# One-hots of the expert slots on two engines, and gate products that start on half of their input

## The reference, cut to what matters

```python
D_MODEL = 1024; N_EXPERT_GROUPS = 4; EXPERTS_PER_GROUP = 8; EXPERT_TOP_K = 2; D_EXPERT = 128
def hier_moe(h, ...):
    pg = softmax(h @ w_rg + b_rg); gi = argmax(pg); gp = pg[gi]
    le_sel = (h @ w_re + b_re).reshape(N, 4, 8)[gi]
    top_p, top_i = lax.top_k(softmax(le_sel), 2)
    top_p = top_p / sum(top_p)
    gates = gp * one_hot(gi) * sum_k(top_p * one_hot(top_i))
    a = einsum('nd,edf->nef', h, w_gate)
    b = einsum('nd,edf->nef', h, w_up)
    hid = silu(a) * b * gates
    return einsum('nef,efd->nd', hid, w_down)
```

## Time and profile before

| | |
|---|---|
| three runs, median | 427.64 us (425.98 to 429.17) |
| profiled execution, its own time | 425.02 us |
| its span | 423.1 us |
| busy: PE | 385.6 us (91%) |
| busy: PEld | 208.2 us (49%) |
| busy: DVE | 214.1 us (51%) |
| busy: ACT | 151.1 us (36%) |
| busy: POOL | 70.4 us (17%) |
| moved by DMA | 109.17 MB, mean 258 GB/s |
| chain that ended last | PE 81%, DVE 8%, DMA 4%, issue 3%, ACT 3% |

### The profile page before, as it was taken

How to read it: one execution, slowest core, us unless ns; L and a number is a source line. 1 busy time by engine, 2 the same in 40 slices (tenths; PEclk the granted TensorE clock), 3 DMA queues, 4 the chain that set the end, 5 groups by cost and what they waited for, 6 DMA issues and landing times.

```text
span 423.1 us, 6421 instructions
## 1 busy us (share of the span) xinstructions
PE 385.6 (91%) x2466; PEld 208.2 (49%) x2466; DVE 214.1 (51%) x442; ACT 151.1 (36%) x321; POOL 70.4 (17%) x59
## 2 busy tenths in 40 slices
PE   0998999979998999999989999879999999998692
PEld 1454544434443434446443466766556555553470
DVE  2967599697457456447361354651212222222276
ACT  5725022222464365454351356312212222222053
POOL 0000546443100100000000001221333233211000
PEclk9999999999999999999999999999999999999698
DMA  8991845892605033960039998999999999995484
GB/s 287 354 279 45 306 136 162 267 352 79 202 0 201 14 114 123 286 214 1 2 104 415 410 412 326 357 352 403 401 409 410 412 408 405 409 394 211 139 323 198
DMA packets 42323, 109.17 MB, mean 258 GB/s; under 512 B 7864, under 2 KB 8632, under 8 KB 42288
## 3 DMA queue, kind: packets, MB, share of 16 engines
q1 hardware_dynamic: 36000, 94.79, 60.7%
q0 software_dynamic: 5856, 12.81, 8.0%
q10 hardware_dynamic: 432, 1.11, 0.8%
HBM read 100.00 MB, written 16.94 MB: 276 GB/s over the span
## 4 chain that ended last, share of the span: by engine, by line
PE 81%; DVE 8%; DMA 4%; issue 3%; ACT 3%; POOLq 0%; DVEq 0%; ACTq 0%
PE bank L1576 34%; PE bank L1890 13%; PE bank L1909 6%; PE bank L1550 4%; PE bank L1879 3%; PE bank L1836 3%; DMA tokens_split<-h_rows,middle 3%; PE bank L1625 3%; PE bank L1617 3%; PE bank L1639 3%; PE bank L1768 2%; PE bank L1672 2%; PE bank L1944 2%; DVE weights_split L1044 2%; PE bank L1699 1%
## 5 line engine op out<-in xcount | busy, mean ns | idle before, releaser
L1576 PE MATMUL bank<-weights_split,tokens_split 128*128 128x512 f16 (+1 forms) x648 | 149.0, 383 | 1.5 <-DVE x L1288 1.4
L1576 PEld LDWEIGHTS bank<-weights_split,tokens_split 128*128 128x128 f16 (+1 forms) x648 | 61.2, 97 | 79.8 <-issue 10.4
L655 POOL TENSOR_TENSOR big<-big,middle 128x1536 f32<-128x1536 f32 x8 | 27.8, 3474 | 64.0 <-DMA middle<-sample_q 41.7
L1890 PE MATMUL bank<-big,tokens_split 128*64 128x256 f32 x320 | 36.7, 382 | 1.5 <-ACT tokens_split L968 1.5
L1471 DVE TENSOR_TENSOR middle<-bank,middle 128x128 f32<-128x128 f32 x16 | 4.7, 292 | 53.7 <-ACT middle L973 53.7
L1890 PEld LDWEIGHTS bank<-big,tokens_split 128*64 128x64 f32 x320 | 23.0, 137 | 12.5 <-ACT tokens_split L968 2.0
L1836 PE MATMUL bank<-half_consts 128*128 128x256 f16 x186 | 23.5, 291 | 4.4 <-issue 4.4
L702 POOL DMA_INDIRECT expert_rows<-weights_split,middle x16 | 16.0, 1002 | 65.9 <-PE bank L1879 42.4
L1550 PE MATMUL bank<-ident,big 128*128 128x128 f32 (+1 forms) x92 | 14.6, 294 | 12.2 <-DVE big L1054 9.5
L844 ACT ACTIVATE middle<-bank 128x128 f32<-128x128 f32 (+3 forms) x32 | 13.9, 435 | 29.5 <-PE bank L1625 29.3
L1836 PEld LDWEIGHTS bank<-half_consts 128*128 128x128 f16 x186 | 19.1, 104 | 8.7 <-issue 5.5
(11 more groups left out here) (199 smaller groups left out, 544.8 us busy)
## 6 DMA issues: line engine op xcount, KB each, us to landing
big<-in_w_gate SPq DMA_DIRECT2D x10, 1024.0 KB, 12.3
big<-in_w_up SPq DMA_DIRECT2D x10, 1024.0 KB, 16.7
big<-in_w_down SPq DMA_DIRECT2D x10, 1024.0 KB, 18.5
middle<-in_w_in SPq DMA_DIRECT2D x16, 512.0 KB, 7.0
big<-in_cache_win_k SPq DMA_DIRECT2D x24, 256.0 KB, 4.5
middle<-in_cache_win_v SPq DMA_DIRECT2D x24, 256.0 KB, 4.5
big<-in_w_out SPq DMA_DIRECT2D x8, 512.0 KB, 7.2
big<-expert_rows SPq DMA_DIRECT2D x8, 512.0 KB, 6.6
```

The costliest lines, as they stand in the source:

```text
L655: nc.gpsimd.tensor_tensor(prod[:, :, :], kring[:, b % 2], qb[:, b % 2, :].unsqueeze(1).to_broadcast([P, NPAT, W]), ALU.mult).then_inc(prod ...
L1576: ins = T.matmul(out, (hT if rows is None else rows)[:, high_low, k if rows is None else k - 4, tokens], wg[:, place, part, k, columns], s ...
L1890: ins = T.matmul((ptb, ovb)[b][e * CAP:(e + 1) * CAP, 0:2 * FE], xT[:, b, k, e * CAP:(e + 1) * CAP], places[slot][:, 0:2, e, k * FE:(k + 1 ...
```

## The change

Four edits belong together.

- **Slot codes.** An odd expert's code is now `1000 * par + rk` (`ODD = 1000`). The row compared with it is 0 to 63 in its first half and 1000 to 1063 in its second. A token with a rank of 64 or more then matches nothing by itself, and the two instructions that added 1000 to it are gone. The row is now written with two instructions in the place of one, during attention.
- **One-hots.** VectorE compares for `kt` = 0 to 6. For 7, 8 and 9 ScalarE computes |code - row| and then max(0, 1 - that), which is 1 where they are equal and 0 elsewhere, since both are whole numbers. The second instruction waits for the first. TensorE's last three small products wait for ScalarE's semaphore.
- **ScalarE's copy** of the first four transposed pieces waits for the fourth transpose (`half_turned`), not for the eighth.
- **Gate products** of chunks 0 to 3 wait for ScalarE's copy only; the wait for VectorE's copy stands ahead of chunk 4.

```diff
+BY_COMPARE, ODD = 7, 1000
...
+            act.wait_ge(slots_ready, 1)
+            for i, kt in enumerate(range(BY_COMPARE, 2 * NT)):
+                hot = onehot_p[:, kt, :]
+                nc.scalar.activation(hot, iota_h, ACT.Abs, scale=-1.0, bias=r1[:, kt:kt + 1]).then_inc(onehots_a, 1)
+                act.wait_ge(onehots_a, 2 * i + 1)
+                nc.scalar.activation(hot, hot, ACT.Relu, scale=-1.0, bias=1.0).then_inc(onehots_a, 1)
+
             def copy_x(n, b):
 
-                act.wait_ge(turned, n + 1)
+                act.wait_ge(half_turned, n + 1)
                 nc.scalar.activation(xT[:, b, 0:4, :], sbk[0][:, :].rearrange("p (k c) -> p k c", k=4),
                                      ACT.Copy).then_inc(xt_a, 1)
...
-                    V.tensor_copy(iota_h, iota[:, 0:P])
+                    V.tensor_copy(iota_h[:, 0:CAP], iota[:, 0:CAP])
+                    V.tensor_scalar(iota_h[:, CAP:P], iota[:, CAP:P], float(ODD - CAP), None, ALU.add)
...
             step(V.tensor_reduce(rk, OX, AX, ALU.add))
-            V.tensor_scalar(r2, rk, float(CAP), 1000.0, ALU.is_ge, ALU.mult)
-            step(V.scalar_tensor_tensor(out=r1, in0=par, scalar=float(CAP), in1=rk, op0=ALU.mult, op1=ALU.add))
-            step(V.tensor_tensor(r1, r1, r2, ALU.add))
+            V.scalar_tensor_tensor(out=r1, in0=par, scalar=float(ODD), in1=rk, op0=ALU.mult,
+                                   op1=ALU.add).then_inc(slots_ready, 1)
+            dve.wait_ge(slots_ready, 1)
 
             def slots():
 
-                for kt in range(2 * NT):
+                for kt in range(BY_COMPARE):
                     V.tensor_scalar(onehot_p[:, kt, :], iota_h, r1[:, kt:kt + 1], None, ALU.is_equal).then_inc(onehots, 1)
...
-                    pe.wait_ge(onehots, kt + 1 if part == 0 else 2 * NT + 1)
+                    if part == 0 and kt >= BY_COMPARE:
+                        pe.wait_ge(onehots_a, 2 * (kt - BY_COMPARE + 1))
+                    else:
+                        pe.wait_ge(onehots, kt + 1 if part == 0 else BY_COMPARE + 1)
...
                 for k in range(KD):
                     ins = T.transpose(sbk[k // 4][:, (k % 4) * P:(k % 4 + 1) * P], xg[:, b, k * P:(k + 1) * P], ident[:, :])
+                    if k == 3:
+                        ins.then_inc(half_turned, 1)
                 ins.then_inc(turned, 1)
 
             def gate_up(base, j):
 
                 n, b, slot = base + j, j % 2, j % SLOTS
                 pe.wait_ge(xt_a, n + 1)
-                pe.wait_ge(xt_d, n + 1)
                 pe.wait_ge(gu_in[slot], base * (2 * LOADS[slot]) + 32 * (j // SLOTS + 1))
                 for k in range(KD):
+                    if k == 4:
+                        pe.wait_ge(xt_d, n + 1)
                     for e in range(2):
```

More of the change, by code:

```diff
@@ L408, in build @@
         zeroed = sem("zeroed")
+        half_turned, slots_ready, onehots_a = sem("half_turned"), sem("slots_ready"), sem("onehots_by_scalar")
         diags_set, rows_gated = sem("diags_set"), sem("rows_gated")
@@ L1429, in more_tables @@
                 step(V.tensor_scalar(hi, xi, 6, None, ALU.logical_shift_right), dv_more)
-                V.scalar_tensor_tensor(out=slot_no, in0=par, scalar=float(CAP), in1=lo, op0=ALU.mult, op1=ALU.add)
+                V.scalar_tensor_tensor(out=slot_no, in0=par, scalar=float(ODD), in1=lo, op0=ALU.mult, op1=ALU.add)
                 step(V.scalar_tensor_tensor(out=r4, in0=hi, scalar=float(PAIRS), in1=pair_no, op0=ALU.mult, op1=ALU.add), dv_more)
```

## The result

Side by side on one chip, 22 runs of each, the changed kernel takes a median of 426.38 us (424.19 to 431.29) and the kernel before 429.13 us (425.34 to 430.75). The ratio is 0.995, with a 95% interval of 0.9927 to 0.9973: 0.5% of 429.13, some 2.1 us less. The two medians themselves lie 2.75 us apart: they count all executions, while every ratio leaves out those over 1.5% above the fastest of their kernel, the slow ones (here two of the changed kernel's, none of the other's). The time lies in the predicted range and within 1%, but the forecast had a gain of 0.2 us. The two profiled executions are 425.02 and 424.58 us, only 0.44 us apart. So there are two questions: why the path gave 0.44 us, and where the other 1.7 us come from. The second is answered in part only.

The account below looks back on a forecast made before the run. The prediction took the router's end as one chain and the full DMA weight stream as holding the last pair: 0.09 at the table and 0.47 made 0.56 us, the stream left 0.25, so 427.64 - 0.2 = 427.4 us, range 425.5 to 429.0.

Parts of the forecast that it names:

- Slot codes and one-hots: Router's end: VectorE's one-hots end at 277.25, ScalarE's last at 277.96, so the table copy starts 0.09 us earlier.
- Rival 2: Router's end: ScalarE's one-hots end after VectorE's did, table 0.29 to 0.6 us later, 427.9 to 428.2 us; chance 0.17.
- The prediction's second estimate: ScalarE's one-hots by the Trainium skill's figures: 0.62 us a one-hot and a table gain of 0.08 us.
- Gate products after half: First two pairs: copying after the fourth transpose starts gate products 0.47 us earlier for pair 0, 0.94 for pair 1.
- What is late next: Gather for pair 3: its issue moves by pair 0's 0.47 only, so TensorE goes on 0.56 us earlier.
- rival 1: Weight stream: it has room, so the first pairs' gain arrives, 0.56 us (427.1) or 1.03 us (426.6); chance 0.26.
- What the stream lets through: Last pair: the weight stream holds its gate products, so 0.25 us of the 0.56 us gain is left.
- TensorE being early adds no byte: Weight stream: after its first loads the DMA engines are full, so the loads move only by the table's 0.09 us.
- The sum: Whole program: profiled execution of 425.02 us less 0.25 us gives 424.8 us.
- The median: Median of three runs, 427.64, lies 2.6 us above the profiled execution most likely through the stream; less 0.2 gives 427.4.
- The likeliest case: Whole program: the forecast itself, with the stream holding the last pair and 427.4 us; chance 0.53.
- the chances by 1%: Whole program: time within 1% (4.3 us) of the kernel before 0.94, faster 0.04, slower 0.02.

Follow-up runs that it names:

- half_only: Kernel before with ScalarE's copy started after the fourth transpose, gate products still waiting for both copies; one run, 425.26 us.
- gates_only: Kernel before with gate products of chunks 0 to 3 waiting for ScalarE's copy only, copies starting as before; one run, 429.01 us.
- light_last: Changed kernel loading only 64 of 1,024 columns of the up-weights of pairs 12 to 15; 427.14 us, ratio 0.9961 to the kernel before.
- before_filler_50: Kernel before with 50 instead of 30 filler products on TensorE between table and first transposes; 426.28 us, ratio 0.9957.
- filler_8: Changed kernel with 8 instead of 30 filler products between table and first transposes; 426.80 us, ratio 0.9985 to the kernel before.
- before_again: Kernel before, unchanged, run once more as its own comparison; 429.65 us, ratio 1.0013; its profiled execution took 429.90 us.
- copies_only: Kernel before with only the copy after the fourth transpose and the later wait ahead of chunk 4, codes and one-hots unchanged; 426.21 us, ratio 0.9954.
- eight_by_vector: Changed kernel with eight one-hots on VectorE and two on ScalarE, instead of seven and three; 428.09 us, ratio 0.9996 to the kernel before.
- codes_only: Changed kernel with ScalarE's copy and the gate products waiting as before, so only codes and one-hots differ; 429.38 us, ratio 0.999 to the kernel before.
- eight_filler_42: Changed kernel with eight one-hots on VectorE, two on ScalarE, and 42 instead of 30 filler products; 424.42 us, ratio 0.9903 to the kernel before.

## Why the prediction was right and wrong

**Slot codes and one-hots: right.** The table was to gain 0.09 us and gained nothing (-0.03). ScalarE as the last engine, its end (277.96 forecast, 278.08 measured) and VectorE's end (277.25, 277.31) came as worked out. Of the 0.12 us between forecast and end, 0.03 are the start (276.08) and 0.09 the six instructions, 2.00 us where 1.91 was taken: a Relu takes 0.31 us, not the copy's 0.272. Rival 2's sign, a last Relu after 278.05, was met by 0.03 us: the table was 0.03 us late, which is nothing, and not the 0.29 to 0.6 of that rival. (The prediction's second estimate, 0.62 us a one-hot, gives by its own terms a gain of 0.06, not 0.08.)

**Gate products after half: right, a little small, and with one term misread.** 0.47 us was forecast for each of the two pairs, 0.54 and 0.55 came. The prediction took the 0.19 us from ScalarE's copy to the products as further passes. They start 0.05 us after the copy now: 0.14 of the 0.19 was the wait for VectorE's copy, which `half_only` and `gates_only` show. For pair 0 it is 0.44 us from the earlier copy and 0.14 from the wait that went, less 0.04 by which the transposes were later. An earlier copy without the second edit did nothing.

**What is late next: right in part.** The wait for the gather of pair 3 grew as forecast (0.62 to 0.99 us), but by 0.37, not 0.47. Its landing moved with its issue and somewhat more (297.39 against 298.10, 0.71), and the next pair got the rest (gate products of pair 3 at 304.87 against 305.89): 1.0 us arrived, the upper end of rival 1.

**What the stream lets through: this step failed.** It said that of 0.56 us only 0.25 is left, since the up-weights of pair 15 land 0.16 us before they are used. No wait for weights appeared, the last pair was 1.0 us earlier, and `light_last` shows that with most of its up-weights left out it starts no closer behind pair 14. The wrong premise is "TensorE being early adds no byte". The loads up to the one at 322.52 wait for gate products, so they moved with TensorE by 1.03 us, and what follows in SP's line moved with them: in the changed kernel the up-weights of pair 15 are issued at 358.14 (359.00 before), take 23.2 us by the profile and land at 381.3, again some 0.16 us ahead of their use. That this landing follows TensorE's pace is read from the order of the code and from two traces; how near the stream really is to holding the last pair is not shown. One more term was off: a pair's bytes are not its weights alone. 128 rows of 4 KB are gathered and as many scattered, which makes 4.2 MB and 10.3 us at 407 GB/s (an estimate), not 7.7.

**The sum.** With the failed step gone the profiled execution should have gained 1.0 us; it gained 0.44. The other 0.56 was lost behind the last pair, at which the prediction did not look: before, the end waits for TensorE's filler and L1944 (0.32 us), with the change for the rows that are read back, whose issue took 0.60 us longer. The 424.8 that was forecast for this execution is 0.2 us off, and by two errors that offset each other: 0.25 us for 1.0 at the last pair, and nothing lost behind it. Whether the 0.56 us is lost in every execution isn't settled by one profile of each.

**The median: the larger miss.** The prediction explained the 2.6 us between the profiled execution and the median of three with the stream. The long executions are those with a lower clock. Of the 91 executions of the kernel before in the three sets of the experiments, 43 had a mean granted clock under 0.98; 42 of them took 429 us or more and the last 428.80. Of the other 48, 8 took 429 us or more. `before_filler_50` shows that an edit that does nothing but keep TensorE at work ahead of the first transposes takes these long executions away, for 0.43% of the time. `filler_8` shows that a fall there is not enough for a long one: in `before_again` only 1.70 of 4.89 us are lost at the first pair, and 1.37 behind the last, where the filler holds up real products. The change does not fill that gap; it shortens the next one, from 0.83 to 0.25 us, and the one ahead of pair 1, from 0.72 us (the bracket of that row in `before_again`) to 0.14 (289.57 less 289.43, the end of the transpose ahead). In its 22 runs 4 reached 429 us, beside it 12 of 22 of the kernel before. So of the 2.1 us 0.4 are the path by the two profiled executions, or up to the 1.0 that the pairs moved if the end doesn't take half of it back; the rest is most likely that fewer executions run at the lower clock. This last step is inferred: no long execution of the changed kernel was profiled, and `copies_only` shows one fall near the first pair (products at 286.84, 5.36 us) with the short gap, so the change may make it rarer and doesn't exclude it.

The likeliest case had 0.53, and its mechanism was wrong. That 426.38 us lies in the range is luck in part: the range was set by the spread of three runs, and the chances by 1% held because the effect is small against that.

**Open:** why the same idle time (1.3 and 0.83 us) is followed by the lower clock in one execution and not in the next; what the falls near 95 us share with those near 285; whether the 0.56 us at the end is lost every time; and what ties the filler ahead of the first pair to the end. From the last gate products to the last VectorE instruction it is 37.63 us in `before_again`, 36.26 in the first profile, 35.41 in `before_filler_50`. Moving or shortening the 100 filler products at the end was not tried.

## What to carry to other kernels

Compare several executions before explaining the median from one profile: look at the granted clock of each, and if the long ones have it lower, find the idle time ahead of the fall. Filling a wait with work that nothing reads can be worth as much as shortening it; but such work must not stand ahead of products that somebody waits for, where a low clock makes it long. An earlier producer is worth little if only the filler ends earlier. And where a wait names one of two producers, take the end times of both; where a landing is just ahead of its use, take the transfer away and see whether the user moves, and ask whether the stream itself was started by the user.

## What the runs showed of the hardware

- TensorE's clock at half (1.2 GHz) near the first pair came for 3.4 us (`before_again`, `copies_only`, `gates_only`, `eight_by_vector`) or 6.8 us (`codes_only`, `filler_8`); 32 products then took 4.57 to 5.61 us instead of 3.67, eight transposes up to 1.97 instead of 1.09. It came after 1.28 us of waiting for the gather in `before_again`, and not after 1.29 in the kernel before nor after 1.76 in `eight_filler_42`.
- A gather issued earlier need not land earlier: 4.86 us from issue to the transposes in `eight_by_vector`, 3.74 in the changed kernel, with weight loads in flight in both.
- On ScalarE an Abs of 128x128 in f16 with a column as bias took 0.38 to 0.40 us, a Relu in place 0.31 us, and the instruction that waits for its forerunner started 0.03 us after its end.
